# Where VectorE makes the low part of a feed-forward tile: before or behind a weight split

## The chip, the cores and the metric

The kernel runs on one core of one Trainium2 chip. The metric is the device time of one execution in microseconds (us). The kernel before takes 809.72 us, the median of 3 runs (809.47 to 810.03).

## The reference

Two layers (DEPTH = 2) of a streaming encoder on x of 256 tokens by 1024 channels, all in float32:

```python
for l in range(DEPTH):
    h = rmsnorm(x, attn_norm_g[l])
    proj = h @ w_in[l]                      # q, k, v, GLU input, two gates
    ...                                     # sliding-window attention and conv branch
    x = x + merged @ w_out[l]
    h = rmsnorm(x, ffn_norm_g[l])
    up = causal_dwconv(h @ w_ffn_up[l], ffn_dw_w[l], ffn_dw_b[l])   # width 3, 2 * 2816 channels
    gt, val = jnp.split(up, 2, axis=-1)
    x = x + (jax.nn.silu(gt) * val) @ w_ffn_down[l]
return rmsnorm(x, final_norm_g)
```

The change lies in the last three lines of a layer, the feed-forward part.

## The kernel before

**Products in three parts.** TensorE works on float32r operands. Every float32 operand is held as a high part (a rounded copy) and a low part (operand minus high part), and a product is the sum of high by high, high by low and low by high. Weights come as units of 128 x 2048 (1 MB). SyncE loads a unit into raw[s], ScalarE copies it to whi[s] (split_high, L326), and VectorE (split_low, L939) or GpSimd (split_low, L267) makes wlo[s] = raw[s] - whi[s]. There are three buffers s = 0, 1, 2. SyncE refills raw[s] once wlo[s] is made (semaphore lo_ready[s]).

**The feed-forward loop.** A layer has 22 tiles of 128 hidden channels, two to a step, so 11 steps. A step j takes three units: the up-projection of its first tile (buffer 2), of its second tile (buffer 0), and the down-projection of two tiles of the step before (buffer 1). In steps 2 to 9 TensorE multiplies the up units "beside" (beside_unit, L1343 and L1349: 512-column products by whi, then 256-column ones by wlo); steps 1 and 10 use plain products (L1084 to L1086), which ask for wlo at their start. The down unit waits for hi_ready[1] and lo_ready[1], then for both parts of its two tiles. In layer 0 its products are L1084 to L1086 with out ps, pt, pc; in layer 1 they are L1372 to L1374.

**One tile on VectorE and ScalarE.** Each engine works off its own list in the order of the code:
- VectorE scale_up: it adds the beside half (L989, waits for ScalarE's copy L583) and scales by rstd into `gate` (L993). In the last step it waits for the unit on TensorE instead.
- ScalarE L588 starts the convolution (two instructions, semaphore f_conv0), then does a split_high, L326.
- VectorE hidden_tile: four taps (L1007), of which the first two wait for f_conv0. ScalarE L593 takes the SiLU. VectorE L1011 multiplies (f_ready).
- ScalarE hidden_high, L597: high part of the tile, fh (named oh in the trace), semaphore fh_ready.
- VectorE hidden_low, L1015: low part, fl (named ol in the trace), semaphore fl_ready. It waits for fh_ready.

Both inputs of L1007, L1011, L1015 and L939 lie in SBUF; L989 and L993 read one input from PSUM. GpSimd's L267 reads raw and whi, both in SBUF.

**Who makes which low weights.** From step 1 on, VectorE makes wlo[2] behind a step's first tile and wlo[0] behind its second. GpSimd makes wlo[1], once per step, as soon as ScalarE has copied whi[1]. ScalarE's order behind a second tile is L597 (the tile's high part), then L326 for whi[1]. GpSimd has nothing else to do in the loop.

**The low part of the second tile** was made at the head of the next step, behind the scale_up of that step's first tile. The last step's second tile got it behind the loop.

Of the kernel before, what the change touches and what calls it, by code (L numbers as in the profile page):

```python
# [12 lines left out]
FT = D_FF // P  # L13
# [61 lines left out]
def hybrid_encoder(nc, x_in, pos_in, const_in, par_in, gf_in, w_in, y_out):  # L75
# [3 lines left out]
    with ctx:  # L79
# [120 lines left out]
        def beside(l, j, ab):  # L200

            return (l * len(BESIDE) + j - BESIDE[0]) * 2 + ab + 1 if j in BESIDE else 0
# [453 lines left out]
        def _(dve):  # L656
# [94 lines left out]
            for l in range(DEPTH):  # L751
# [184 lines left out]
                def split_low(s, n):  # L936

                    dve.wait_ge(hi_ready[s], hi_count(l * USES + n))
                    V.tensor_tensor(wlo[s][:, :], raw[s][:, :], whi[s][:, :].bitcast(f32), ALU.subtract).then_inc(lo_ready[s], 1)  # L939
# [43 lines left out]
                def scale_up(s, ab, done_value, beside=0):  # L983

                    total = four[:, 2 * ab, :, :]
                    if beside:
                        total = four[:, 2 * ab:2 * ab + 2, 0, :]
                        dve.wait_ge(up_low, beside)
                        V.tensor_tensor(total, total, up_lows[ab], ALU.add).then_inc(up_sum, 1)  # L989
                        dve.wait_ge(up_sum, beside)  # L990
                    else:
                        dve.wait_ge(unit_done[s], done_value)
                    V.tensor_tensor(up[:, ab, :, :], total, rstd[:, :].unsqueeze(1).to_broadcast([P, 2, T]),  # L993
                                    ALU.mult).then_inc(up_ready, 1)

                def hidden_tile(k, ab, gcol, vcol):

                    for m in range(4):
                        half, tap = m % 2, 1 - m // 2
                        shift = 2 - tap  # L1000
                        if m < 2:
                            dve.wait_ge(f_conv0, k * 2 + 2)
                        else:
                            dve.wait_ge(f_tap, k * 4 + m - 1)
                        col = (gcol, vcol)[half] + tap
                        acc = fbuf[:, ab, half, shift:T]
                        last = V.scalar_tensor_tensor(acc, up[:, ab, half, 0:T - shift], par[:, col:col + 1], acc,  # L1007
                                                      ALU.mult, ALU.add).then_inc(f_tap, 1)
                    dve.wait_ge(f_tap, k * 4 + 4)
                    dve.wait_ge(f_silu, k + 1)  # L1010
                    V.scalar_tensor_tensor(fbuf[:, ab, 3, :], fbuf[:, ab, 2, :], 1.0, fbuf[:, ab, 1, :], ALU.mult, ALU.mult).then_inc(f_ready, 1)  # L1011

                def hidden_low(k, ab, parity):
                    dve.wait_ge(fh_ready, k + 1)
                    V.scalar_tensor_tensor(fl[:, 2 * parity + ab, :], fbuf[:, ab, 3, :], 1.0, fh[:, 2 * parity + ab, :].bitcast(f32),  # L1015
                                           ALU.mult, ALU.subtract).then_inc(fl_ready, 1)

                k0 = l * FT
# [8 lines left out]
                def ffn_step(j, parity, last):  # L1027
                    k = j * 2 + l * FT
                    col = j * 8 + PA_FW
                    scale_up(2, 0, l * USES + j + 11, beside(l, j, 0))  # L1030
                    hidden_low(k - 1, 1, 1 - parity)
                    hidden_tile(k, 0, col, col + FT * 4)
                    split_low(2, j + 11)
                    scale_up(0, 1, l * USES + j + 12, beside(l, j, 1))
                    hidden_low(k, 0, parity)
                    hidden_tile(k + 1, 1, col + 4, col + FT * 4 + 4)
                    if not last:
                        split_low(0, j + 12)

                for r in range(FFN_STEPS // 2 - 1):  # L1040
                    ffn_step(r * 2 + 1, 1, False)
                    ffn_step(r * 2 + 2, 0, False)
                ffn_step(FFN_STEPS - 2, 1, False)
                ffn_step(FFN_STEPS - 1, 0, True)
                hidden_low(k0 + FT - 1, 1, 0)

                if l < DEPTH - 1:
                    for i in range(4):
# [458 lines left out]
```

## Time and profile before

| | |
|---|---|
| median of 3 runs | 809.72 us (809.47 to 810.03) |
| the profiled execution: its time | 809.75 us |
| the profiled execution: its span, first to last instruction | 807.9 us |
| mean granted TensorE clock | 0.999 |
| feed-forward loop of layer 0, first to last GpSimd split | 253.49 to 391.99 us |
| feed-forward loop of layer 1, first to last GpSimd split | 649.85 to 788.32 us |

The 1.8 us between span and time lie around the instructions. Times inside the trace are us from the span's start. A row of the timeline has a start, a length, the engine, the line, the operation, out<-in by name with shapes, and a count of merged instructions. Behind them, in brackets, stands how long the engine sat idle before and what ended that. A length is counted to the end of the instruction's record, so it also holds time in which the instruction had been issued and could not proceed. Two neighbours can overlap by some hundredths of a microsecond.

### The profile page before, as it was taken

What the parts mean: (1) busy time and instruction counts of PE and PEld (TensorE: products, weight loads), DVE (VectorE), ACT (ScalarE), POOL (GpSimd) and SP (SyncE); (2) the same over time, 40 slices, a digit from 0 to 9 for tenths busy, and PEclk for the clock granted to TensorE, in tenths of its full rate; (3) what the DMA queues carried; (4) which work ended last, traced back from release to release, by engine and by line L of the source; (5) the groups of instructions that cost most, each with busy time, mean ns of one, the idle gap of its engine ahead of it and who ended that gap; (6) DMA issues with size and microseconds to landing.
All of it is one profiled execution on the core that took longest, in us unless ns stands there. A gap on an engine that the chain in (4) does not pass through costs nothing.

```text
span 807.9 us, 15118 instructions
## 1 busy us (share of the span) xinstructions
PE 795.4 (98%) x6042; PEld 748.7 (93%) x6042; DVE 623.6 (77%) x1181; ACT 536.6 (66%) x890; POOL 455.2 (56%) x139
## 2 busy tenths in 40 slices
PE   8999999999999999999999999999999999999996
PEld 8999989899999999999999999989999988888895
DVE  5899999673458888887779999885434777887885
ACT  6858978773666665656676577887446565656664
POOL 6999678778722223322389987787786023222240
PEclk9999999999999999999999999999999999999999
DMA  8655434445445545555455544434555445555441
GB/s 301 234 190 196 157 113 150 157 164 197 162 169 196 191 174 183 189 203 203 163 183 184 197 159 167 150 113 157 180 212 183 164 176 198 180 198 206 157 157 52
DMA packets 21381, 142.69 MB, mean 177 GB/s; under 512 B 2496, under 2 KB 3008, under 8 KB 4672
## 3 DMA queue, kind: packets, MB, share of 16 engines
q1 hardware_dynamic: 20736, 140.69, 49.4%
q10 hardware_dynamic: 576, 1.04, 0.4%
q8 instruction: 48, 0.79, 0.4%
q14 instruction: 21, 0.17, 0.1%
HBM read 140.68 MB, written 1.05 MB: 175 GB/s over the span
## 4 chain that ended last, share of the span: by engine, by line
PE 87%; DVE 7%; ACT 3%; DMA 1%; issue 1%; SPq 0%; DVEq 0%; ACTq 0%
PE four L1084 16%; PE four L1086 15%; PE four L1085 15%; PE four L1343 15%; PE four L1349 8%; DVE pc L780 3%; PE ps L1084 1%; PE ps L1085 1%; PE ps L1086 1%; PE ps L1372 1%; PE ps L1373 1%; PE ps L1374 1%; PE four L1218 1%; DVE ol L1015 1%; DMA x<-in_x_t 1%; PE ps L1196 1%
## 5 line engine op out<-in xcount | busy, mean ns | idle before, releaser
L267 POOL TENSOR_TENSOR wlo<-raw,whi 128x2048 fp32r<-128x2048 f32 x86 | 397.5, 4627 | 326.0 <-ACT whi L326 315.7
L326 ACT ACTIVATE whi<-raw 128x2048 fp32r<-128x2048 f32 x129 | 245.9, 1906 | 9.6 <-PE four L1086 9.6
L1084 PE MATMUL four<-hh,whi 128*128 128x256 f32 x704 | 201.4, 286 | 0.0
L1086 PE MATMUL four<-hh,wlo 128*128 128x256 f32 x704 | 199.2, 283 | 0.0
L1085 PE MATMUL four<-hl,whi 128*128 128x256 f32 x704 | 199.1, 283 | 0.0
L780 DVE SCALAR_TENSOR_TENSOR pc<-upad,par_all,pc 128x256 f32<-128x256 f32 x404 | 162.8, 481 | 0.1
L1084 PEld LDWEIGHTS four<-hh,whi 128*128 128x128 f32 x704 | 134.9, 192 | 5.2 <-issue 5.2
L1085 PEld LDWEIGHTS four<-hl,whi 128*128 128x128 f32 x704 | 135.0, 192 | 0.0
L1086 PEld LDWEIGHTS four<-hh,wlo 128*128 128x128 f32 x704 | 135.0, 192 | 0.0
L1343 PE MATMUL four<-u_both,whi 128*128 128x512 f32 x512 | 128.0, 392 | 0.0
L1343 PEld LDWEIGHTS four<-u_both,whi 128*128 128x128 f32 x512 | 92.6, 189 | 16.9
L588 ACT ACTIVATE qk<-gate,par_all 128x256 f32<-128x256 f32 x88 | 48.2, 595 | 88.9 <-DVE gate L993 88.9
L1084 PE MATMUL four<-u_both,whi 128*128 128x256 f32 x368 | 104.6, 284 | 0.0
L1086 PE MATMUL four<-u_both,wlo 128*128 128x256 f32 x368 | 104.1, 283 | 0.0
L1085 PE MATMUL four<-u_both,whi 128*128 128x256 f32 x368 | 104.1, 283 | 0.0
L939 DVE TENSOR_TENSOR wlo<-raw,whi 128x2048 fp32r<-128x2048 f32 x42 | 95.9, 2284 | 0.0
L1007 DVE SCALAR_TENSOR_TENSOR qk<-gate,par_all,qk 128x254 f32<-128x254 f32 (+1 forms) x176 | 73.1, 476 | 22.3 <-ACT qk L588 22.3
L1349 PEld LDWEIGHTS four<-u_both,wlo 128*128 128x128 f32 x512 | 69.8, 190 | 5.0
L1349 PE MATMUL four<-u_both,wlo 128*128 128x256 f32 x512 | 71.4, 282 | 0.0
L1085 PEld LDWEIGHTS four<-u_both,whi 128*128 128x128 f32 x368 | 70.6, 192 | 0.1
L1084 PEld LDWEIGHTS four<-u_both,whi 128*128 128x128 f32 x368 | 70.6, 192 | 0.1
L1086 PEld LDWEIGHTS four<-u_both,wlo 128*128 128x128 f32 x368 | 70.6, 192 | 0.0
(240 smaller groups left out, 1367.5 us busy)
## 6 DMA issues: line engine op xcount, KB each, us to landing
raw<-in_weights SPq DMA_DIRECT2D x130, 1024.0 KB, 4.8
raw<-in_weights SPq DMA_DIRECT2D x3, 512.0 KB, 7.8
out_y<-qk SPq DMA_DIRECT2D x3, 256.0 KB, 2.4
x<-in_x_t SPq DMA_DIRECT2D x2, 256.0 KB, 4.0
raw<-in_weights SPq DMA_DIRECT2D x2, 256.0 KB, 3.8
x<-in_x_t SPq DMA_DIRECT2D x1, 512.0 KB, 7.0
gate<-in_final_g ACTq DMA_DIRECT2D x1, 512.0 KB, 4.0
out_y<-qk ACTq DMA_DIRECT2D x1, 256.0 KB, 2.9
```

The costliest lines, as they stand in the source:

```text
L267: nc.gpsimd.tensor_tensor(wlo[s][:, :], raw[s][:, :], whi[s][:, :].bitcast(f32), ALU.subtract).then_inc(lo_ready[s], 1)
L326: A(whi[s][:, :], raw[s][:, :], ACT.Copy).then_inc(hi_ready[s], 1)
L588: A(fbuf[:, ab, half, :], up[:, ab, half, :], ACT.Identity, scale=par[:, col + 2:col + 2 + 1], bias=par[:, col + 3:col + 3 + 1]).then_inc( ...
L780: V.scalar_tensor_tensor(out, upad[:, t, k:k + T], w, sums, ALU.mult, ALU.add).then_inc(conv_step, 1)
L939: V.tensor_tensor(wlo[s][:, :], raw[s][:, :], whi[s][:, :].bitcast(f32), ALU.subtract).then_inc(lo_ready[s], 1)
L1007: last = V.scalar_tensor_tensor(acc, up[:, ab, half, 0:T - shift], par[:, col:col + 1], acc, ALU.mult, ALU.add).then_inc(f_tap, 1)
L1015: V.scalar_tensor_tensor(fl[:, 2 * parity + ab, :], fbuf[:, ab, 3, :], 1.0, fh[:, 2 * parity + ab, :].bitcast(f32), ALU.mult, ALU.subtract ...
L1084: MM(out, whi[s][:, w], hi, start=start, stop=False, skip_group_check=accumulate)
L1085: MM(out, whi[s][:, w], lo, start=False, stop=False, skip_group_check=accumulate)
L1086: return MM(out, wlo[s][:, w], hi, start=False, stop=stop, skip_group_check=accumulate)
L1343: MM(four[:, first + m, :, :].rearrange("p a t -> p (a t)"), whi[s][:, w], u_both[:, k, :, :].rearrange("p a t -> p (a t)"), start=(k == 0 ...
L1349: last = MM(four[:, first + m, 1, :], wlo[s][:, w], uh[:, k, :], start=False, stop=(k == NT - 1), skip_group_check=True)
```

## The change

VectorE's hidden_low for a step's second tile moves from the head of the next step to directly behind the tile, ahead of the split_low of buffer 0. Step 1 keeps the hidden_low at its head, for the second tile of the part in front of the loop. The call behind the loop goes, as the last step now makes its own.

```diff
                     scale_up(2, 0, l * USES + j + 11, beside(l, j, 0))
-                    hidden_low(k - 1, 1, 1 - parity)
+                    if j == 1:
+                        hidden_low(k - 1, 1, 1 - parity)
                     hidden_tile(k, 0, col, col + FT * 4)
                     split_low(2, j + 11)
                     scale_up(0, 1, l * USES + j + 12, beside(l, j, 1))
                     hidden_low(k, 0, parity)
                     hidden_tile(k + 1, 1, col + 4, col + FT * 4 + 4)
+                    hidden_low(k + 1, 1, parity)
                     if not last:
                         split_low(0, j + 12)
 
@@ -1042,7 +1044,6 @@
                 ffn_step(FFN_STEPS - 2, 1, False)
                 ffn_step(FFN_STEPS - 1, 0, True)
-                hidden_low(k0 + FT - 1, 1, 0)
```

VectorE, the end of one step inside the loop and the head of the next, before (a name's number is its buffer; what a row waits for stands in brackets):

```order
L1007 SCALAR_TENSOR_TENSOR qk<-gate,par_all,qk 128x254 [waits f_tap] x2
L1011 SCALAR_TENSOR_TENSOR qk<-qk 128x256 [waits f_silu,f_tap]
L939 TENSOR_TENSOR wlo0<-raw0,whi0 128x2048 [waits hi_ready0]
L989 TENSOR_TENSOR four<-four,gate 128x2x256 [waits up_low]
L993 TENSOR_TENSOR gate<-four,rstd 128x512 [waits up_sum]
L1015 SCALAR_TENSOR_TENSOR ol<-qk,oh 128x256 [waits fh_ready]
L1007 SCALAR_TENSOR_TENSOR qk<-gate,par_all,qk 128x255 [waits f_conv0] x2
```

The same place with the change:

```order
L1007 SCALAR_TENSOR_TENSOR qk<-gate,par_all,qk 128x254 [waits f_tap] x2
L1011 SCALAR_TENSOR_TENSOR qk<-qk 128x256 [waits f_silu,f_tap]
L1015 SCALAR_TENSOR_TENSOR ol<-qk,oh 128x256 [waits fh_ready]
L939 TENSOR_TENSOR wlo0<-raw0,whi0 128x2048 [waits hi_ready0]
L989 TENSOR_TENSOR four<-four,gate 128x2x256 [waits up_low]
L993 TENSOR_TENSOR gate<-four,rstd 128x512 [waits up_sum]
L1007 SCALAR_TENSOR_TENSOR qk<-gate,par_all,qk 128x255 [waits f_conv0] x2
```

L1015 with its wait for fh_ready now stands ahead of the split L939, not behind L993. This happens at nine places of each layer, behind the second tiles of steps 1 to 9; at the head of the last step L993 waits for unit_done2 and there is no L989. The lists of GpSimd and ScalarE and TensorE's instructions stay what they were.

## Rows read from the trace of the kernel before

**Rows 1.** The page: busy time by engine, and the chain by engine

```profile
PE 795.4 (98%) x6042; PEld 748.7 (93%) x6042; DVE 623.6 (77%) x1181; ACT 536.6 (66%) x890; POOL 455.2 (56%) x139
...
PE 87%; DVE 7%; ACT 3%; DMA 1%; issue 1%; SPq 0%; DVEq 0%; ACTq 0%
```

**Rows 2.** Timeline of PE: first product of a down unit, both layers

```profile
258.58 0.28 PE L1084 MATMUL ps<-oh,whi 128*128 128x256 f32 x1
...
343.25 0.28 PE L1084 MATMUL ps<-oh,whi 128*128 128x256 f32 x1
...
656.38 0.40 PE L1372 MATMUL ps<-whi,oh 128*128 128x512 f32 x1
...
772.67 0.40 PE L1372 MATMUL ps<-whi,oh 128*128 128x512 f32 x1
```

**Rows 3.** Timeline of PE: its idle time in the last products of each layer

```profile
402.08 0.36 PE L1084 MATMUL ps<-oh,whi 128*128 128x256 f32 x1 [1.05 <-DVE ol L1015]
...
798.05 0.47 PE L1372 MATMUL ps<-whi,oh 128*128 128x512 f32 x1 [1.41 <-DVE ol L1015]
```

**Rows 4.** Timeline of POOL: splits of the feed-forward loops, both layers

```profile
253.49 4.63 POOL L267 TENSOR_TENSOR wlo<-raw,whi 128x2048 fp32r<-128x2048 f32 x1 [26.54 <-ACT whi L326]
...
337.19 4.62 POOL L267 TENSOR_TENSOR wlo<-raw,whi 128x2048 fp32r<-128x2048 f32 x1 [12.16 <-ACT whi L326]
353.92 4.63 POOL L267 TENSOR_TENSOR wlo<-raw,whi 128x2048 fp32r<-128x2048 f32 x1 [12.11 <-ACT whi L326]
...
387.36 4.63 POOL L267 TENSOR_TENSOR wlo<-raw,whi 128x2048 fp32r<-128x2048 f32 x1 [12.09 <-ACT whi L326]
...
649.85 4.63 POOL L267 TENSOR_TENSOR wlo<-raw,whi 128x2048 fp32r<-128x2048 f32 x1 [26.59 <-ACT whi L326]
...
783.69 4.63 POOL L267 TENSOR_TENSOR wlo<-raw,whi 128x2048 fp32r<-128x2048 f32 x1 [12.10 <-ACT whi L326]
```

**Rows 5.** Tile ol on DVE: count, then shortest, median and longest in ns

```profile
L1015 DVE SCALAR_TENSOR_TENSOR ol<-qk,oh x44: 412/416/3901, 234.1 to 797.5; 128x256 fp32r<-128x256 f32 x44
```

**Rows 6.** Timeline of DVE, one turn of the loop in layer 0

```profile
339.83 2.26 DVE L1015 SCALAR_TENSOR_TENSOR ol<-qk,oh 128x256 fp32r<-128x256 f32 x1
342.02 1.66 DVE L1007 SCALAR_TENSOR_TENSOR qk<-gate,par_all,qk 128x255 f32<-128x255 f32 x4
...
351.15 0.43 DVE L1011 SCALAR_TENSOR_TENSOR qk<-qk 128x256 f32<-128x256 f32 x1 [0.52 <-ACT qk L593]
351.50 2.28 DVE L939 TENSOR_TENSOR wlo<-raw,whi 128x2048 fp32r<-128x2048 f32 x1
```

**Rows 7.** Timeline of ACT, the end of the same turn

```profile
351.61 0.42 ACT L597 ACTIVATE oh<-qk 128x256 fp32r<-128x256 f32 x1 [0.57 <-DVE qk L1011]
351.94 1.90 ACT L326 ACTIVATE whi<-raw 128x2048 fp32r<-128x2048 f32 x1
```

**Rows 8.** Timeline of DVE, the last tile of layer 0

```profile
400.60 0.42 DVE L1011 SCALAR_TENSOR_TENSOR qk<-qk 128x256 f32<-128x256 f32 x1 [0.52 <-ACT qk L593]
401.50 0.43 DVE L1015 SCALAR_TENSOR_TENSOR ol<-qk,oh 128x256 fp32r<-128x256 f32 x1 [0.48 <-ACT oh L597]
```

**Rows 9.** Timeline of DVE, step 1 of layer 0: the split of buffer 0

```profile
251.07 2.28 DVE L939 TENSOR_TENSOR wlo<-raw,whi 128x2048 fp32r<-128x2048 f32 x1
```

**Rows 10.** DMA issues: count, KB each, median us to landing

```profile
raw<-in_weights SPq DMA_DIRECT2D x130, 1024.0 KB, 4.8
```

**Rows 11.** Timelines of ACT and DVE, head of step 9, layer 0

```profile
373.82 1.10 ACT L588 ACTIVATE qk<-gate,par_all 128x256 f32<-128x256 f32 x2 [1.49 <-DVE gate L993]
...
375.47 1.65 DVE L1007 SCALAR_TENSOR_TENSOR qk<-gate,par_all,qk 128x255 f32<-128x255 f32 x4
```

**Rows 12.** The same in layer 1

```profile
769.38 1.09 ACT L588 ACTIVATE qk<-gate,par_all 128x256 f32<-128x256 f32 x2 [1.49 <-DVE gate L993]
...
771.79 1.65 DVE L1007 SCALAR_TENSOR_TENSOR qk<-gate,par_all,qk 128x255 f32<-128x255 f32 x4
```

## The prediction

> **What bounds the kernel now.** The page comes first: TensorE is busy for 98% and holds 87% of the chain of waits [rows 1]. That suggests that a VectorE instruction can move freely. So I asked where TensorE is idle. In the feed-forward loop its down units start 16.93 us apart in layer 0 (258.58 to 343.25 is five turns) and 16.61 us apart in layer 1 (656.38 to 772.67, seven turns) [rows 2]. The only pauses are at the very end of a layer, 1.05 and 1.41 us, both ended by VectorE's L1015, the last tile's low part [rows 3]. So each layer's end hangs on VectorE, and the question is what paces VectorE through the loop.
>
> GpSimd's timeline shows it. Nine splits stand in each layer, and from the first to the last are eight turns of 16.73 us: 253.49 to 387.36, and 649.85 to 783.69 [rows 4]. It is the same number in both layers, although TensorE's turns differ, so this turn isn't TensorE's. It closes like this. L1015 at the head of a step takes 2.26 us where its median is 0.416 [rows 5, 6]. It ends at 342.09, and GpSimd's split ran from 337.19 to 341.81 [rows 4]: VectorE stood still until GpSimd was done. From there VectorE does its two tiles, ScalarE's L597 and then the copy of whi[1] follow the second L1011, that copy ends at 353.84 [rows 7], and GpSimd starts at 353.92. The loop is GpSimd end, VectorE's two tiles, ScalarE's copy, GpSimd. In layer 0 it is 0.2 us shorter than TensorE's turn, in layer 1 it is 0.12 longer, and TensorE's slack absorbs that until the end.
>
> **The change part by part.** Per layer nine L1015 move. None is added, no DMA is issued otherwise, and ScalarE's and GpSimd's lists are the same.
>
> *The head of steps 2 to 10.* L1015 goes from there. It doesn't take its 2 us of standing still along: next in line is L1007, which also has two SBUF inputs, and ScalarE's L588 is ready before GpSimd ends in these steps. The first tap will stand still in its place and end with GpSimd. What is saved is one place in the queue. For a 256-column instruction that is 0.35 us, as between the starts of L1011 and L939 (351.15, 351.50) [rows 6].
>
> *The tail of steps 1 to 9.* L1015 now follows L1011 at once and must wait for ScalarE's L597. The last tile of the layer already does that: 400.60 to 401.50, so 0.90 us from start to start, 0.48 of it idle [rows 8]. The instruction behind, the split of buffer 0, had started 0.35 behind L1011 and now starts 0.90 + 0.35 behind it: 0.90 later.
>
> *Whom the split meets.* Before, that split ended at 353.78 and GpSimd's began at 353.92 [rows 4, 6]: they just missed each other. With the change a turn that begins at the same GpSimd end of 341.81 has its split end at 353.78 - 0.35 + 0.90 = 354.33. ScalarE's copy comes 0.35 earlier, near 353.49, so GpSimd now asks while VectorE's split is in the middle of its run. The trace has only the other order, VectorE waiting for GpSimd. No row shows GpSimd waiting for VectorE, since the nine splits are all 4.62 to 4.63 long. I take the exclusion to be mutual, because an instruction that stands still until the other's end shows a lock on something both need, not a share of bandwidth. The Trainium skill says so outright: by its page "SBUF — State Buffer", section "Who interferes with whom", a VectorE instruction with two SBUF inputs and a GpSimd instruction that reads SBUF shut each other out, and whichever comes second waits for the whole of the first. Of this case's rows one direction agrees, the other isn't shown.
>
> *The gap g* between VectorE's end and GpSimd's start is unknown. Lower end: L1015's own 0.41 us fits between 341.68 and 342.09, so it began 0.13 before GpSimd's recorded end, and the mirror gives g = -0.13 [rows 4, 6]. Upper end: GpSimd starts 0.08 behind the ScalarE copy that releases it, g = +0.08 [rows 4, 7]. Both are equally near to the case, so I take the middle, -0.025, and keep the ends for the range. The skill's same page, section "A bandwidth-pool intuition that's wrong (but worth ruling out)", measured about 115 ns behind VectorE's end for another kind of GpSimd work; with g = 0.115 the sum below would be 9.5 us, 819.2 us in all, and no row here shows it.
>
> *Sum for a layer.* The first GpSimd split moves from 253.49 to 251.07 + 2.28 + 0.90 = 254.25, plus g: 0.76 + g later [rows 4, 9]. There is no saving ahead of it, as step 1 keeps its head. Each of the eight turns grows by 354.33 - 353.92 = 0.41 + g, and the last head saves 0.35. Together 0.76 + 8 x 0.41 - 0.35 + 9g = 3.69 + 9g, for two layers 7.38 + 18g. With g = -0.025 this is 6.9 us; the ends are 5.0 and 8.8. The turn becomes 17.12 us, longer than TensorE's in either layer.
>
> *Is it on the path?* Behind the last GpSimd end the program is the same except for the 0.35, and VectorE's last L1015 ends each layer, so a late GpSimd moves the end one for one. TensorE has no way to hide it. Its down unit needs wlo[1]: in layer 0 GpSimd's first end, 258.12, was 0.46 ahead of the unit's start at 258.58, in layer 1 654.48 was 1.9 ahead [rows 2, 4]. Layer 0 uses that up with the first split and is then late by 0.2 every turn, layer 1 loses 0.5 a turn and is late from the fourth or so. TensorE then takes GpSimd's pace and waits at the head of the down unit.
>
> *What else moves.* The low part of the second tile is ready about 6 us earlier, which nobody waits for. SyncE reloads raw[0] 0.9 us later and raw[1] with GpSimd; a load lands 4.8 us behind its issue [rows 10], and ScalarE reads it some ten us behind the issue, so I cost this at nothing. If that cover went, a ScalarE copy would wait for a DMA. The split of buffer 0 is wanted by TensorE only halfway through the first part of its unit, but the last step asks at its start: there TensorE may wait some tenths, beside VectorE's path.
>
> The profiled execution took 809.75 us, the median is 809.72. Forecast: 809.75 + 6.9 = **816.7 us**.
>
> **The rivals.**
>
> *A, faster: the exclusion works one way.* GpSimd starts when ScalarE's copy is ready, whatever VectorE runs. Then the turn is 16.73 - 0.35 = 16.38, shorter than TensorE's, and VectorE follows TensorE. In step 9 of layer 0 the taps could begin when L588 ends, 374.92, and not at 375.47 (0.55 earlier) [rows 11]; with the last head's 0.35 that is 0.9 us. In layer 1 it is 771.79 - 770.47 = 1.32, plus 0.35, capped by TensorE's idle 1.41 [rows 3, 12]. Sum 2.3 us: 807.4 us. It decides if g is under -0.41, where the turn stops growing. For it speaks that no row shows GpSimd held up. Against it, VectorE's long rows end with GpSimd's to a few hundredths. I give 9%. If instead L1007 didn't stand still, the gain would be TensorE's whole idle, 1.05 + 1.41: 807.3 us, 3%.
>
> *B, no change: GpSimd gets in early.* VectorE's split lets go well ahead of its recorded end, by about 0.4 us. Then a turn keeps its 16.73, and the first split's 0.35 is given back by the last head: 809.8 us, 4%. That the page's 98% for TensorE hides everything would give the same time, but the two idle rows speak against it.
>
> *C, slower still.* GpSimd is kept out longer, or VectorE slips a further place each turn. With g = +0.15 it is 10.1 us, 819.8. I count this in the forecast's own range.
>
> **How the numbers follow.** The forecast's mechanism has 84%, and its own range is 5.0 to 8.8 us widened by some 1.2 us either way for turns that don't repeat exactly: 813.6 to 820.0. A and its variant have 12%, B 4%. They are left out of the range, which leaves about 2 in 10 outside. A measurement here tells a change from none at about 0.2%, 1.6 us. Faster by more: 0.12; within: 0.04; slower: 0.84.
>
> **What would show it.** In the new profile GpSimd's nine splits should stand 17.0 to 17.2 us apart in both layers. GpSimd should begin, or its row be drawn out to over 5 us, as VectorE's split of buffer 0 ends. VectorE's long row should be L1007 at a head, with L1015 0.42 everywhere and 0.48 idle before each second one. TensorE should be idle at the first product of down units, released by GpSimd's wlo. It is wrong if GpSimd starts inside VectorE's split with 4.62 us (rival A), if the turn stays 16.73 (B), or if L1007 runs at normal length under a GpSimd split.

## The result and the profile after

The changed kernel takes 813.91 us (median of 6 runs, 813.61 to 814.33), the kernel before 809.72: 4.2 us more, ratio 1.0052 with a 95% interval of 1.0039 to 1.0065. The profiled execution took 814.33 us with a span of 812.5, so 4.6 us more than the one shown of before. Three executions of two kernels further down took 958 to 2735 us, and the ratios leave these out.

The page barely tells. Busy time and the chain by engine:

```profile
PE 797.7 (98%) x6042; PEld 749.6 (92%) x6042; DVE 620.1 (76%) x1181; ACT 536.2 (66%) x890; POOL 466.8 (57%) x139
...
PE 54%; DVE 28%; ACT 12%; issue 3%; DMA 1%; SPq 0%; DVEq 0%; ACTq 0%
```

TensorE is still busy for 98%. Two numbers have moved: GpSimd (POOL) is "busy" for 466.8 us and not 455.2 with the same 139 instructions [rows 1], and the chain has gone from TensorE's 87% to 54%, with VectorE and ScalarE at 40% together. GpSimd has no share of the chain: time in which an instruction stands still lies inside the length of its row, so the chain counts VectorE's standing still to VectorE. Now the timeline of GpSimd, where rows 4 stood before:

```profile
253.62 5.26 POOL L267 TENSOR_TENSOR wlo<-raw,whi 128x2048 fp32r<-128x2048 f32 x1 [26.56 <-ACT whi L326]
...
338.53 5.28 POOL L267 TENSOR_TENSOR wlo<-raw,whi 128x2048 fp32r<-128x2048 f32 x1 [11.76 <-ACT whi L326]
355.53 5.25 POOL L267 TENSOR_TENSOR wlo<-raw,whi 128x2048 fp32r<-128x2048 f32 x1 [11.72 <-ACT whi L326]
...
389.46 5.26 POOL L267 TENSOR_TENSOR wlo<-raw,whi 128x2048 fp32r<-128x2048 f32 x1 [11.70 <-ACT whi L326]
...
652.17 5.26 POOL L267 TENSOR_TENSOR wlo<-raw,whi 128x2048 fp32r<-128x2048 f32 x1 [26.59 <-ACT whi L326]
...
787.96 5.28 POOL L267 TENSOR_TENSOR wlo<-raw,whi 128x2048 fp32r<-128x2048 f32 x1 [11.71 <-ACT whi L326]
```

The same instruction is 5.26 us long, 0.63 more than in rows 4, eighteen times: that is nearly all of GpSimd's 11.6 us of extra "busy". It begins on ScalarE's release and stands still. From first to last are 135.84 and 135.79 us over eight turns, 16.98 and 16.97 us a turn where it was 16.73. VectorE in one turn, which answers to rows 6 (here and below the changed kernel's timeline):

```profile
341.81 3.47 DVE L1007 SCALAR_TENSOR_TENSOR qk<-gate,par_all,qk 128x255 f32<-128x255 f32 x4 [1.16 <-ACT qk L588]
...
352.76 0.43 DVE L1011 SCALAR_TENSOR_TENSOR qk<-qk 128x256 f32<-128x256 f32 x1 [0.52 <-ACT qk L593]
353.68 0.43 DVE L1015 SCALAR_TENSOR_TENSOR ol<-qk,oh 128x256 fp32r<-128x256 f32 x1 [0.49 <-ACT oh L597]
354.02 2.29 DVE L939 TENSOR_TENSOR wlo<-raw,whi 128x2048 fp32r<-128x2048 f32 x1
```

VectorE's split now runs from 354.02 to 356.31. GpSimd's row begins at 355.53 and ends at 360.78; its own 4.63 us fit in from 356.15. At the head the four taps take 3.47 us and not 1.66: they stand still in the low part's place. The low part is short everywhere, which answers to rows 5. So is L989, which reads one input from PSUM and often runs under a GpSimd split, as it does here at 356.22:

```profile
L1015 DVE SCALAR_TENSOR_TENSOR ol<-qk,oh x44: 412/416/428, 234.3 to 802.0; 128x256 fp32r<-128x256 f32 x44
L989 DVE TENSOR_TENSOR four<-four,gate x32: 690/692/700, 254.3 to 780.4; 128x512 f32<-128x512 f32 x32
```

TensorE in layer 0, the first down unit (rows 2), the second unit of the last step, and the last products (rows 3):

```profile
258.98 0.36 PE L1085 MATMUL ps<-oh,whi 128*128 128x256 f32 x1
...
390.38 0.36 PE L1085 MATMUL four<-u_both,whi 128*128 128x256 f32 x1 [0.77 <-DVE wlo L939]
...
404.40 0.36 PE L1085 MATMUL ps<-oh,whi 128*128 128x256 f32 x1 [1.56 <-DVE ol L1015]
```

and in layer 1 the first products of the down units of steps 8 and 9, the second unit of the last step, and the last products:

```profile
759.37 0.47 PE L1373 MATMUL ps<-whi,oh 128*128 128x512 f32 x1
...
776.36 0.47 PE L1373 MATMUL ps<-whi,oh 128*128 128x512 f32 x1
...
788.89 0.36 PE L1085 MATMUL four<-u_both,whi 128*128 128x256 f32 x1 [1.05 <-DVE wlo L939]
802.58 0.47 PE L1373 MATMUL ps<-whi,oh 128*128 128x512 f32 x1 [0.89 <-DVE ol L1015]
```

The down unit starts 0.10 us behind GpSimd's first end (258.88), and the two units in layer 1 are 16.99 us apart. The rows of the down units show no idle time in brackets, but their starts follow GpSimd's ends: 0.10 to 0.14 us behind them in steps 2 to 9 of layer 0, and 0.10 to 0.11 behind from step 6 on in layer 1. TensorE still pauses at both layer ends for VectorE's last low part, 1.56 and 0.89 us, so the lateness was not absorbed there. ScalarE waits for no DMA in either feed-forward loop, so the later reloads cost nothing, as forecast.

### The profile page after: what moved, and what is told of

The parts are those of the page before. It is cut to its first block, busy times and chain, and to the rows that moved or that the text cites. A ratio compares the mean times of both kernels' runs of the same rounds, so it can differ in the third digit from the quotient of the medians.

```text
span 812.5 us, 15118 instructions
## 1 busy us (share of the span) xinstructions
PE 797.7 (98%) x6042; PEld 749.6 (92%) x6042; DVE 620.1 (76%) x1181; ACT 536.2 (66%) x890; POOL 466.8 (57%) x139
## 3 DMA queue, kind: packets, MB, share of 16 engines
HBM read 140.68 MB, written 1.05 MB: 174 GB/s over the span
## 4 chain that ended last, share of the span: by engine, by line
PE 54%; DVE 28%; ACT 12%; issue 3%; DMA 1%; SPq 0%; DVEq 0%; ACTq 0%
PE four L1085 14%; PE four L1086 14%; PE four L1087 14%; DVE wlo L939 9%; DVE qk L1007 6%; ACT whi L326 5%; DVE pc L780 3%; DVE gate L993 3%; ACT qk L588 3%; PE four L1344 2%; DVE four L989 2%; DVE qk L1011 2%; ACT qk L593 2%; PE four L1350 1%; PE four L1219 1%
## 5 line engine op out<-in xcount | busy, mean ns | idle before, releaser
L267 POOL TENSOR_TENSOR wlo<-raw,whi 128x2048 fp32r<-128x2048 f32 x86 | 409.0, 4760 | 319.2 <-ACT whi L326 309.4
L1007 DVE SCALAR_TENSOR_TENSOR qk<-gate,par_all,qk 128x254 f32<-128x254 f32 (+1 forms) x176 | 104.9, 656 | 43.2 <-ACT qk L588 43.2
L1344 PEld LDWEIGHTS four<-u_both,whi 128*128 128x128 f32 x512 | 92.6, 189 | 16.9
L939 DVE TENSOR_TENSOR wlo<-raw,whi 128x2048 fp32r<-128x2048 f32 x42 | 96.0, 2285 | 0.0
```

The source lines that it names most:

```text
L267: nc.gpsimd.tensor_tensor(wlo[s][:, :], raw[s][:, :], whi[s][:, :].bitcast(f32), ALU.subtract).then_inc(lo_ready[s], 1)
L1344: MM(four[:, first + m, :, :].rearrange("p a t -> p (a t)"), whi[s][:, w], u_both[:, k, :, :].rearrange("p a t -> p (a t)"), start=(k == 0 ...
```

## The experiments

My theory: GpSimd, VectorE and ScalarE wait for each other in a circle, which the prediction calls a loop. It sets VectorE's pace in both feed-forward loops before, and with the change TensorE's too. GpSimd's split and a VectorE instruction with two SBUF inputs shut each other out. The change costs because VectorE's split of buffer 0, late by the 0.48 us of waiting and by one instruction more ahead of it in the list, holds GpSimd up in every turn. The rivals: the low part's new place costs by itself on VectorE, or VectorE's work alone sets the pace. Eight kernels, each against the kernel before on the chip that it ran on. The kernel before took 809.7 us on each of these chips, so the times can be compared with each other.

**The low part behind the split.** It still moves ahead of the next head, but the split doesn't wait for it:

```diff
                     hidden_tile(k + 1, 1, col + 4, col + FT * 4 + 4)
-                    hidden_low(k + 1, 1, parity)
                     if not last:
                         split_low(0, j + 12)
+                    hidden_low(k + 1, 1, parity)
```

> The second tile's low part stands behind VectorE's split of buffer 0 and still ahead of the next step's head. My theory (a loop GpSimd, VectorE, ScalarE, in which each holds up the next) says: the split is not late any more, the head still saves its 0.40 us, the low part slips in between the split and GpSimd's start and delays GpSimd by about 0.1 us. The turn would be about 16.4 us, shorter than TensorE's, so TensorE paces the loop and both layer ends move up by up to their idle 1.05 and 1.41 us: 807.5 us, GpSimd's rows about 4.7 us long. Rival 1: the early place of the low part itself costs, whatever the split does: 812 or more. Rival 2: GpSimd gets the port first and VectorE stands still for its whole split ahead of the scale-up; the turn would grow by about 2 us, some 845 us.

Measured: 807.95 us, ratio 0.9976 (0.9967 to 0.9985). It is faster than both kernels. GpSimd's timeline:

```profile
253.59 4.69 POOL L267 TENSOR_TENSOR wlo<-raw,whi 128x2048 fp32r<-128x2048 f32 x1 [26.55 <-ACT whi L326]
...
302.78 4.68 POOL L267 TENSOR_TENSOR wlo<-raw,whi 128x2048 fp32r<-128x2048 f32 x1 [11.71 <-ACT whi L326]
319.56 4.69 POOL L267 TENSOR_TENSOR wlo<-raw,whi 128x2048 fp32r<-128x2048 f32 x1 [12.10 <-ACT whi L326]
...
387.29 4.69 POOL L267 TENSOR_TENSOR wlo<-raw,whi 128x2048 fp32r<-128x2048 f32 x1 [12.25 <-ACT whi L326]
```

The first three turns are 16.40 us each (253.59 to 302.78): the circle at its own pace. Then TensorE's 16.9 rules, as the longer idle time in the brackets shows. At the end of layer 0 TensorE's pause is down to 0.56 us, from 1.05 [rows 3], and at the end of layer 1 to 0.17, from 1.41; together that is the 1.7 us gained:

```profile
401.68 0.36 PE L1085 MATMUL ps<-oh,whi 128*128 128x256 f32 x1 [0.56 <-DVE ol L1015]
...
796.42 0.47 PE L1373 MATMUL ps<-whi,oh 128*128 128x512 f32 x1 [0.17 <-DVE ol L1015]
```

VectorE, same kernel:

```profile
351.01 2.28 DVE L939 TENSOR_TENSOR wlo<-raw,whi 128x2048 fp32r<-128x2048 f32 x1
353.21 0.42 DVE L1015 SCALAR_TENSOR_TENSOR ol<-qk,oh 128x256 fp32r<-128x256 f32 x1
```

The low part needs no waiting there (ScalarE was done during the split), and it costs GpSimd 0.06 us (4.69 against 4.63). So the low part's early time is free; rival 1 falls.

**The same place as in the change, without the wait.** Left out is the second tile's low part in steps 1 to 9: the instruction reads the SiLU half and rstd.

```diff
-                    hidden_low(k + 1, 1, parity)
+                    if last:
+                        hidden_low(k + 1, 1, parity)
+                    else:
+                        V.scalar_tensor_tensor(fl[:, 2 * parity + 1, :], fbuf[:, 1, 2, :], 1.0, rstd[:, :],
+                                               ALU.mult, ALU.subtract).then_inc(fl_ready, 1)
```

> The changed order, but in steps 1 to 9 the second tile's low part reads other data (the SiLU half and rstd) and so doesn't wait for ScalarE; its values are not the reference's. My theory: the split of buffer 0 is late by one queue place, 0.35 us, and that is what the head saved; GpSimd isn't held up (rows 4.6 to 4.7 us), the turn is 16.3 to 16.4 us, and TensorE paces the loop: 807.5 us. Rival (the place in the queue costs, not the wait): 812 to 814 us as the change.

Measured: 807.93 us, ratio 0.9976 (0.9966 to 0.9985), GpSimd's rows 4.67 to 4.71 long, as this one:

```profile
353.27 4.68 POOL L267 TENSOR_TENSOR wlo<-raw,whi 128x2048 fp32r<-128x2048 f32 x1 [12.19 <-ACT whi L326]
```

The instruction's place costs nothing that the time shows. What makes the change slower is the wait, with the split queued behind it.

**One and two extra instructions ahead of the split**, in the old order:

```diff
                     if not last:
+                        for _ in range(1):
+                            V.tensor_tensor(kr[:, _, :], rstd[:, :], rstd[:, :], ALU.mult)
                         split_low(0, j + 12)
```

> The order before, with one extra 256-column VectorE instruction (0.35 us to the next, no wait, a scratch output) ahead of each split of buffer 0. My theory has a threshold: the split then ends 0.35 later, 0.21 behind GpSimd's old start, and GpSimd begins in effect 0.13 ahead of the split's end; 0.08 us a turn, 18 turns: 1.4 us, 811.1 us. Rival (VectorE's own work paces the loop, every 0.35 counts): 6.3 us, 816.0. Rival (TensorE paces, the lateness is hidden): 809.7.

> The same with two extra instructions, 0.70 us. My theory: 0.43 us a turn beyond the threshold, 18 turns: 7.7 us, 817.5 us; GpSimd's rows about 5.1 us long. Rival (VectorE's own work paces the loop): 12.6 us, 822.3. Rival (TensorE paces): 809.7 to 811.

Measured: 810.73 us with one (ratio 1.0011, 1.0002 to 1.0019) and 816.73 with two (1.0088, 1.0075 to 1.0101). The first instruction (0.34 us) costs 1.0 us in all, the second 6.0: a threshold, as a meeting of two instructions gives it and a plain sum of VectorE's work doesn't. GpSimd's timelines, with one:

```profile
337.42 4.68 POOL L267 TENSOR_TENSOR wlo<-raw,whi 128x2048 fp32r<-128x2048 f32 x1 [12.11 <-ACT whi L326]
354.20 4.68 POOL L267 TENSOR_TENSOR wlo<-raw,whi 128x2048 fp32r<-128x2048 f32 x1 [12.10 <-ACT whi L326]
```

and with two:

```profile
339.01 5.03 POOL L267 TENSOR_TENSOR wlo<-raw,whi 128x2048 fp32r<-128x2048 f32 x1 [12.11 <-ACT whi L326]
356.14 5.03 POOL L267 TENSOR_TENSOR wlo<-raw,whi 128x2048 fp32r<-128x2048 f32 x1 [12.10 <-ACT whi L326]
```

Turns of 16.78 and 17.13 us: each is 12.10 us of idle time for GpSimd plus the row. Only the row's length changes.

**GpSimd's split cut to half**, in both orders. Left out is the second half of the low part of the down weights in steps 2 to 10, where old values stay.

```diff
                 for n in range(13, USES):
-                    split_low(1, l * USES + n)
+                    pool.wait_ge(hi_ready[1], hi_count(l * USES + n))
+                    nc.gpsimd.tensor_tensor(wlo[1][:, 0:1024], raw[1][:, 0:1024], whi[1][:, 0:1024].bitcast(f32), ALU.subtract).then_inc(lo_ready[1], 1)
```

> The order before, with GpSimd's split of buffer 1 in steps 2 to 10 cut to its first 1024 columns: half the low part of those down weights is left out (stale values). GpSimd then runs about 2.4 us and is done before VectorE's low part at the head asks. My theory: no instruction stands still, TensorE paces the loop, the layer ends keep at most a few tenths of idle: 807.5 us. Rival (VectorE and ScalarE pace the loop by themselves, GpSimd only happens to run beside): 809.7.

> The changed order with the same halved GpSimd split (the same part left out). The split of buffer 0 still ends 0.9 us later than in the order before, and GpSimd may still be held for some tenths, but it ends long before the taps ask. My theory: the whole cost of the change goes, 807.5 us, within 0.5 of the halved kernel in the old order. Rival (the wait for ScalarE costs on VectorE's own path): 4 us more than that kernel, 811.5.

Measured: 806.83 us in the old order (0.9964, 0.9950 to 0.9978), 807.02 in the changed one (0.9964, 0.9952 to 0.9977). The change's 4.2 us are gone. GpSimd, old order, then changed order:

```profile
336.49 2.40 POOL L312 TENSOR_TENSOR wlo<-raw,whi 128x1024 fp32r<-128x1024 f32 x1 [14.59 <-ACT whi L327]
```

```profile
336.60 3.03 POOL L312 TENSOR_TENSOR wlo<-raw,whi 128x1024 fp32r<-128x1024 f32 x1 [13.97 <-ACT whi L327]
```

It is still held up by 0.63 us in the changed order, and VectorE still waits for ScalarE. Neither costs anything when VectorE's next taps don't have to stand still until GpSimd's end. Both times lie 0.5 to 0.7 below what I expected; TensorE's timeline has no pause left in either feed-forward loop, where I had expected a few tenths.

**One more instruction at the head of the changed kernel**, where the low part had stood, in steps 2 to 10: once with two SBUF inputs, once a memset.

```diff
                     if j == 1:
                         hidden_low(k - 1, 1, 1 - parity)
+                    else:
+                        V.tensor_tensor(kr[:, 0, :], rstd[:, :], rstd[:, :], ALU.mult)
```

```diff
+                    else:
+                        V.memset(kr[:, 0, :], 0.0)
```

> The changed order with one extra 256-column VectorE instruction with two SBUF inputs (scratch output, no wait) at the head of steps 2 to 10, where the low part stood before. My theory: it stands still in place of the first tap, and the taps lose the queue place that the change had saved, 0.40 us in each of 9 turns and 2 layers: 813.9 + 7.2 = 821.1 us; turn 17.4 us. Rival (it fits into VectorE's idle 1.16 us ahead of the taps and costs nothing): 813.9.

> The same place, but the extra instruction is a memset of the same 256 columns, which has no input. My theory: it doesn't stand still under GpSimd's split and fits into the idle 1.16 us ahead of the taps: 813.9 us, its row under 0.5 us. Rival (GpSimd keeps VectorE off SBUF altogether, or any instruction at this place costs its queue place): 819 to 821.

Measured: 821.97 us (1.0150, 1.0135 to 1.0165) and 813.82 us (1.0051, 1.0036 to 1.0066). VectorE's timeline with the two inputs, and then with the memset:

```profile
342.40 3.52 DVE L1034 TENSOR_TENSOR kr<-rstd 128x256 f32<-128x256 f32 x1
345.84 0.47 DVE L1007 SCALAR_TENSOR_TENSOR qk<-gate,par_all,qk 128x255 f32<-128x255 f32 x1
```

```profile
340.06 0.27 DVE L1034 MEMSET kr<- 128x256 f32 x1
341.23 3.46 DVE L1007 SCALAR_TENSOR_TENSOR qk<-gate,par_all,qk 128x255 f32<-128x255 f32 x4 [0.89 <-ACT qk L588]
```

Both are issued under a running GpSimd split, at a place where VectorE in the changed kernel had 1.16 us of idle time ahead of its taps. The one with SBUF inputs is 3.52 us long, nearly all of it standing still, and costs 8.1 us over the change; the memset takes 0.27 and costs nothing. This also prices what the change saves at the head: with the extra instruction GpSimd's idle time is 12.10 us a turn again and not 11.71, so one instruction there is worth 0.39 us a turn, 7.0 us in all. The profiled execution (821.24) is 6.9 above the changed kernel's; the rest of the 8.1 between the medians is not explained.

## Why the prediction was right, step by step

**How right.** The direction and the mechanism were right, the size only roughly: 4.2 us against 6.9. The mechanism's own sum went from 5.0 to 8.8 us. The measured cost lies under it, and is inside the range (813.6 to 820.0) only by the 1.2 us of margin; with this margin the upper end should have been 819.8. The term that was mis-sized is g.

**The circle** shows in GpSimd's idle time between two splits. Where it sets the pace, that is 12.10 us in the old order, with none, one or two extra instructions ahead of the split, and 11.71 in the changed order; the length of the row is what varies besides. Cutting GpSimd's work brought TensorE's turns back, 16.93 and 16.61 us. Read straight from these rows, the change costs a layer 0.63 for the first split, 1.97 for eight turns (135.84 - 133.87) and -0.39 for the last head: 2.2 us, 4.4 in two layers.

**The mutual exclusion**, which the trace of before showed in one direction only, is real in the other: GpSimd's rows are drawn out to 5.26 us, and to 3.03 when halved. The Trainium skill's page "SBUF — State Buffer", section "Who interferes with whom", states that two SBUF inputs on VectorE and a GpSimd read of SBUF exclude each other, and that VectorE doesn't contend with at most one SBUF input outside its 2-port modes. This case agrees: GpSimd's rows are drawn out by 0.63 us, while the memset and L989 keep their length. Rival A needed the opposite and falls; its variant falls with the first tap, which stood still as forecast.

**The gap g** is where the forecast was too high. I took the middle of -0.13 and +0.08. The rows above give 356.15 - 356.31 = -0.16. In the step before the first turn (step 1 of layer 0) VectorE's split stands as

```profile
252.11 2.28 DVE L939 TENSOR_TENSOR wlo<-raw,whi 128x2048 fp32r<-128x2048 f32 x1
```

so g is 258.88 - 4.63 - 254.39 = -0.14. I take -0.15. The mirror of VectorE's own blocked row (-0.13) was nearly right, the release by a semaphore (+0.08) was not; why a held instruction begins this early, no run shows. Against -0.025 that is 18 x 0.125 = 2.3 us of the 2.8 by which 816.7 was over. The Trainium skill's page "SBUF — State Buffer", section "A bandwidth-pool intuition that's wrong (but worth ruling out)", gives about 115 ns behind VectorE's end for GpSimd's writing of DMA descriptors; this GpSimd split doesn't follow it, with its -0.14 to -0.16.

**The head's saving** was a little larger than the 0.35: behind GpSimd's end VectorE's taps are done 1.47 us later and not 1.87 (345.28 - 343.81 against 343.68 - 341.81 [rows 4, 6]), so 0.40. Nine times in two layers this is another 0.9 us off. The two corrections give 7.38 - 18 x 0.15 - 18 x 0.05 = 3.8 us; measured were 4.2.

**The tail's delay** of 0.90 was right to 0.02 (352.76 to 353.68 is 0.92, in other turns 0.91); over 18 places that is another 0.2 to 0.4 us, about what is missing. **TensorE** takes GpSimd's pace: its turns in layer 1 grow from 16.61 to 16.99 us, but from step 6 on, the fifth unit and not the fourth, as a turn grew by less than forecast. The idle time that I had named as a sign, at the first product of the down units, is too short to be printed; the units start right behind GpSimd's ends. TensorE also waits 0.77 and 1.05 us in the last steps for VectorE's split, "some tenths" in my text, and VectorE's path still ends last. **Rival B** (no change) would have needed g near -0.4.

## What to carry to other kernels

A wait placed ahead of a long instruction delays that instruction and everything that must stay clear of it; the same short work placed behind the long one here found its input ready and was worth 6 us between the two places. When two engines' instructions just miss each other in the trace (here by 0.14 us), that is a threshold: price a shift by what lies beyond it, and multiply by the turns. The room was in fact 0.14 + 0.15 = 0.29 us, since a held instruction begins before the other's recorded end: an instruction of 0.34 us ahead of the split drew GpSimd's row out by only 0.05. An engine that is busy for 98% doesn't prove that it sets the pace: compare the turn lengths of each engine across stages.

## What the hardware showed beyond what I had expected

A held instruction ends as if it had begun 0.13 to 0.16 us before the holder's recorded end and then run at its usual length, in both directions: VectorE behind GpSimd (-0.13), and GpSimd behind VectorE (-0.14 and -0.16; also when its split is halved, 3.03 us against 2.40). The profile counts the standing still as busy time: in the changed kernel GpSimd's share of the span rose from 56% to 57% and it did no more work.
